# Fused transformer stack on one core: weight roundings issued one product earlier in attention, and units' steps put ahead of mixed rows' splits in the third layer

## The chip, the cores and the metric

One core of a Trainium2 chip. The metric is the device time of one execution in microseconds (us). Each kernel is run several times; the median is compared.

## The reference

Two blocks in sequence on 256 rows of width 1024, float32. The first has four layers of the kinds A, B, C, A:

```
q, k, v, (indexer), qm = x @ w_in
mix   = attention(rope(q), rope(k), v)      # A: top-64 keys by an indexer, B: dilated, C: causal
mo    = memory_attention(qm, mem_n @ w_mem_kv)
mixed = concat([mix, mo]) @ w_out
x     = layer_norm(ALPHA * x + mixed)
x     = layer_norm(ALPHA * x + swiglu(x, w_gate_up, w_down))
```

The second block has two layers of retention and stick-breaking attention. The change touches the attention of the four layers of the first block alone. They are called layer one to four here (0 to 3 in the code).

## The kernel before

A planner (class Plan) writes one list of steps; each engine's program then walks that list and issues its own part of each step. So the order of the list is the order on every engine, and every engine works strictly along its own queue, waiting on semaphores.

**Products.** Weights come as tiles of 128 x 2048 (half of the contraction for 512 output columns). A product is one tile against one block of 128 rows: 12 matmuls (L1309; L1303 and L1306 for transposed kinds), in three passes: rounded weights times rounded rows, rounded weights times the rows' remainder, the weights' remainder times rounded rows. Two halves make one result in a PSUM bank of a ring of two (`gemms`), which is then copied out: L1560 on ScalarE (ACT), L1920 on VectorE (DVE), by the `by` given in `some` (layer four copies the rows' values on ACT alone).

**Weights.** SyncE fetches tiles into three places of `w_raw`. Two steps make a tile usable. `high` (L1528, ACT) rounds it to `w_high`; `low` (L1777, DVE) writes the remainder `w_low`. `w_high` and `w_low` have five places each, so `high` of a tile waits for the last product of the tile five before it. `low` is cut in two where a unit's scores follow within one product (function `around`): the first half is L1777, the rest (`low_rest`, L1784) comes just after the step that masks the scores.

**Bookkeeping.** `owed` counts places that may be refilled now; `given_back` counts places that came free but are only added to `owed` at the next `split` or `settle`. A product that is `prompt` adds its place to `owed` at once. `split` issues the pending `low` steps and one `high`; `ahead` issues one `high`; `on` advances the background units and calls `split`.

**Units.** Attention runs as units of some heads on one block of 128 rows, advanced in the background between products, pipelined three deep. A unit's steps: scores (PE L1163); mask and maximum (DVE L2061, for memory L2039); exponentials (ACT L1604, L1612); reciprocals (DVE L2075); division of half of the heads on ACT (L1623) and half on DVE (L2085; the dilated kind adds three parts at L2078 and L2080 instead); transposition of the probabilities (PE L1376) into a ring of two PSUM banks (`tr`); copies of them to SBUF (DVE L2099); weighted sum of values (PE L1410 or L1402), which takes a bank of the same ring; its copy out (ACT L1648, dilated: DVE L2117). In the text the units of rows 0 are A0, B0 and M0 (memory), those of rows 1 are C1, C2, C3 (in layer two also C4) and M1.

**Mixed rows' split.** Before the output product the mixed rows are split into rounded rows and remainder: `mix_split`, ACT L1655 and DVE L2106, in halves (group 0 and group 1) for each block of rows. Layer two transposes them on PE first (L1238, L1537, L1811).

The order of products in `attention` and `out_and_forward` (layer three): values' last columns and memory queries, values' columns for rows 0 and rows 1 (`some`), then the output weights, four tiles W0 to W3 (columns 0 and 512 of the first half, then of the second), rows 0 then rows 1, then the first gate/up tile G0. Layers one and four have the memory queries between the values' products.

```
while self.used.get(self.oldest) == RB or ...:
    back = self.tiles[self.oldest].name != "w_ada_2"
    self.given_back, self.owed = self.given_back + (back and not prompt), self.owed + (back and prompt)
```

Of the kernel before, what the change touches and what calls it, by code (L numbers as in the profile page):

```python
# [150 lines left out]
class Plan:  # L151
# [624 lines left out]
    def attention(self, layer, gen, keys, values, tail):  # L776


        kind, mix = KINDS[layer], ("mix", layer)
        own = [self.own_units(layer, rb) for rb in range(RB)]  # L780
        mem = [self.memory_unit(layer, rb) for rb in range(RB)]
        ahead = 1 if kind == "A" else 0
        units = self.headed(own[0] + own[1][:ahead] + mem[:1] + own[1][ahead:] + mem[1:], 1)

        def begin():
            self.held = False
            self.on()
            self.drain()
            self.beside(units)
            self.step_background()  # L790

        def keys_turned(rb):
            def then():
                self.background[:] = [self.abreast(self.turn_heads(layer, "k", rb, 2 if kind == "A" and rb == 0 else 1),
                                                   *self.background)]
                self.step_background() if late else self.on()
            return then
        late = kind == "A" and layer
        self.group([keys], gen, [[self.on, keys_turned(0)], [self.step_background if late else self.on, keys_turned(1)]], True)
        if kind == "A":  # L800
            t = [self.tile(*values[:4], 4 * half) for half in range(2)]
            t_tail = [self.tile(tail[0], tail[1], None, "queries", 0)] * 2
        else:
            t_tail, t = [[self.tile(*what[:4], 4 * half) for half in range(2)] for what in (tail, values)]

        def some(n, tiles, where, sort, hooks):
            use = self.gemms.take()
            for half in range(2):
                self.gemm(tiles[half], n, half, gen, "gemm", use, sort)
                if half:  # L810
                    by = ("dve",) * 2 if where[0] == "qm" else ("act",) * 2 if where == ("proj", LAST, 3) else ("act", "dve")
                    self.evacuate(where, by=by)(n, use, tiles[half])
                hooks[half]()
            return use
        if kind != "A":
            self.blocks[("qm", layer), 0] = some(1, t_tail, ("tail", layer), "tail", [self.on, begin])
        some(0, t, ("proj", layer, 3), "block", [begin if kind == "A" else self.on, self.on])
        if kind == "A":
            some(0, t_tail, ("qm", layer), "queries", [self.on_ahead if layer == LAST else self.on, self.on])
        else:  # L820
            use = some(0, t_tail, ("tail", layer), "tail", [self.on] * 2)
            for rb in range(RB):
                self.blocks[("v", layer), rb] = use

        def first_turned():
            if kind == "A":
                self.step_background()
            self.xt(mix, 0, (0,))
            if kind == "C":
                self.on_ahead()  # L830
            else:
                self.split() if kind == "A" else self.on()

        def turned():
            if kind == "C":
                self.low_one()
            if kind != "A":
                assert len(self.units[layer, 0]) == len(own[0]) + 1
                self.xt(mix, 0, (1,))
            self.on()  # L840
        some(1, t, ("proj", layer, 3), "block", [first_turned, turned])

    def out_and_forward(self, layer):
# [2027 lines left out]
```

## Time and profile before

| | |
|---|---|
| median of 3 runs | 1554.36 us (1553.69 to 1554.85) |
| profiled execution | 1553.68 us |
| its span, first to last instruction | 1551.9 us |
| busy in the span: PE, DVE, ACT | 1528.5, 1088.2, 760.7 us |
| granted TensorE clock, mean | 0.999 |

Read the busy time of PE first, then where PE waits inside the attention stretches, then which engine's instruction ends each wait. An instruction's own time is the column after its start; the number in brackets is how long its engine had been idle before it and what ended that. Consecutive instructions of one engine can overlap by some 0.1 us, so the time that one takes from its engine is the distance between starts.

### The profile page before, as it was taken

What the parts mean: (1) busy time and instruction counts of PE and PEld (TensorE: products, weight loads), DVE (VectorE), ACT (ScalarE), POOL (GpSimd) and SP (SyncE); (2) the same over time, 40 slices, a digit from 0 to 9 for tenths busy, and PEclk for the clock granted to TensorE, in tenths of its full rate; (3) what the DMA queues carried; (4) which work ended last, traced back from release to release, by engine and by line L of the source; (5) the groups of instructions that cost most, each with busy time, mean ns of one, the idle gap of its engine ahead of it and who ended that gap; (6) DMA issues with size and microseconds to landing.
All of it is one profiled execution on the core that took longest, in us unless ns stands there. A gap on an engine that the chain in (4) does not pass through costs nothing.

```text
span 1551.9 us, 19840 instructions
## 1 busy us (share of the span) xinstructions
PE 1528.5 (98%) x8091; PEld 1267.8 (82%) x8091; DVE 1088.2 (70%) x1561; ACT 760.7 (49%) x963; POOL 52.1 (3%) x89
## 2 busy tenths in 40 slices
PE   9999999999999999999999999999999999999997
PEld 7887788888878888888788888877888888978986
DVE  6986866656777775676966756888667678567764
ACT  5657444444445443346544343566444434574463
POOL 1100000000000000000000000000100000000010
PEclk9999999999999999999999999999999999999999
DMA  8661666644435766352476654533766645433530
GB/s 320 245 231 55 226 224 264 249 174 179 163 104 201 262 261 243 138 215 83 178 252 234 244 225 148 204 109 136 267 257 236 223 166 223 164 118 140 217 122 27
DMA packets 45898, 299.87 MB, mean 193 GB/s; under 512 B 5540, under 2 KB 5796, under 8 KB 12528
## 3 DMA queue, kind: packets, MB, share of 16 engines
q1 hardware_dynamic: 39600, 278.74, 48.6%
q0 software_dynamic: 5776, 19.01, 3.7%
q8 instruction: 64, 1.05, 0.3%
q10 hardware_dynamic: 432, 0.85, 0.1%
q14 instruction: 26, 0.21, 0.0%
HBM read 296.20 MB, written 2.65 MB: 193 GB/s over the span
## 4 chain that ended last, share of the span: by engine, by line
PE 83%; DVE 9%; ACT 4%; issue 2%; DMA 0%; POOL 0%; POOLq 0%; SPq 0%; DVEq 0%; ACTq 0%
PE psum L1309 53%; PE psum L1268 15%; PE psum L1303 7%; DVE w_low L1777 3%; PE psum L1163 2%; PE psum L1238 1%; PE psum L1422 1%; ACT work L1604 1%; PE psum L1325 1%; ACT w_high L1528 1%; PE psum L1306 1%; DVE work L2061 1%; PE psum L1376 1%; DVE work L2099 1%; DVE xt_low L1811 0%
## 5 line engine op out<-in xcount | busy, mean ns | idle before, releaser
L1528 ACT ACTIVATE w_high<-w_raw 128x2048 fp32r<-128x2048 f32 (+1 forms) x240 | 456.4, 1903 | 230.7 <-DMA w_raw<-in_weights 144.9
L1777 DVE TENSOR_TENSOR w_low<-w_raw,w_high 128x2048 fp32r<-128x2048 f32 (+2 forms) x240 | 530.0, 2214 | 34.4 <-ACT w_high L1528 33.3
L1309 PE MATMUL psum<-w_high,xt_high 128*128 128x512 f32 (+1 forms) x1376 | 378.6, 395 | 1.4 <-DVE x_rows L1875 0.7
L1309 PE MATMUL psum<-w_high,xt_low 128*128 128x512 f32 (+1 forms) x1376 | 368.4, 388 | 0.3 <-DVE xt_low L1811 0.3
L1309 PE MATMUL psum<-w_low,xt_high 128*128 128x512 f32 (+1 forms) x1376 | 368.1, 388 | 0.0
L1309 PEld LDWEIGHTS psum<-w_high,xt_low 128*128 128x128 f32 x1376 | 257.4, 188 | 54.8 <-DVE xt_low L1811 0.7
L1309 PEld LDWEIGHTS psum<-w_low,xt_high 128*128 128x128 f32 x1376 | 257.3, 188 | 53.7 <-DVE w_low L1777 0.4
L1309 PEld LDWEIGHTS psum<-w_high,xt_high 128*128 128x128 f32 x1376 | 249.8, 188 | 52.5 <-DVE x_rows L1875 2.3
L2128 DVE TENSOR_TENSOR arena<-arena,psum 128x256 f32<-128x256 f32 x88 | 36.9, 420 | 205.4 <-ACT arena L1663 205.0
L1663 ACT ACTIVATE arena<-psum 128x256 f32<-128x256 f32 x88 | 33.7, 383 | 218.5 <-PE psum L1309 218.5
L1268 PE MATMUL psum<-w_high,ht_high 128*128 128x512 f32 x352 | 99.9, 401 | 0.0
L1268 PE MATMUL psum<-w_high,ht_low 128*128 128x512 f32 x352 | 96.1, 390 | 0.0
L1268 PE MATMUL psum<-w_low,ht_high 128*128 128x512 f32 x352 | 95.9, 390 | 0.0
L1268 PEld LDWEIGHTS psum<-w_high,ht_low 128*128 128x128 f32 x352 | 66.1, 188 | 14.4
L1268 PEld LDWEIGHTS psum<-w_low,ht_high 128*128 128x128 f32 x352 | 66.1, 188 | 14.1
L1268 PEld LDWEIGHTS psum<-w_high,ht_high 128*128 128x128 f32 x352 | 63.2, 188 | 11.0
L1560 ACT ACTIVATE arena<-psum 128x512 f32<-128x512 f32 (+1 forms) x54 | 30.4, 569 | 83.0 <-PE psum L1309 46.3
L1800 DVE SCALAR_TENSOR_TENSOR arena<-w_raw,c_col,arena 128x512 f32<-128x512 f32 x84 | 62.9, 749 | 2.6
L2364 POOL TENSOR_TENSOR norm_rstd<-norm_rstd,half_neg 128x1 f32<-128x1 f32 (+1 forms) x32 | 22.8, 715 | 1126.8 <-DVE norm_rstd L1860 871.2
L1604 ACT ACTIVATE work<-work,neg_max 128x128 f32<-128x128 f32 (+3 forms) x80 | 38.0, 477 | 28.2 <-DVE neg_max L2061 27.9
L1920 DVE TENSOR_SCALAR arena<-psum 128x512 f32<-128x512 f32 x25 | 17.2, 688 | 48.3 <-PE psum L1309 25.4
L1811 DVE TENSOR_TENSOR xt_low<-psum,xt_high 128x512 fp32r<-128x512 f32 (+1 forms) x48 | 31.0, 672 | 18.0 <-ACT xt_high L1537 17.5
(253 smaller groups left out, 1494.8 us busy)
## 6 DMA issues: line engine op xcount, KB each, us to landing
w_raw<-in_weights SPq DMA_DIRECT2D x260, 1024.0 KB, 4.8
norm_params<-in_ln_g POOLq DMA_DIRECT2D x8, 512.0 KB, 4.4
norm_params<-in_ln_b POOLq DMA_DIRECT2D x8, 512.0 KB, 5.9
w_raw<-in_weights SPq DMA_DIRECT2D x4, 656.0 KB, 6.1
kv_outside<-arena POOLq DMA_DIRECT2D x3, 512.0 KB, 4.5
mem_kv<-kv_outside POOLq DMA_DIRECT2D x3, 512.0 KB, 3.7
norm_params<-mods_outside POOLq DMA_DIRECT2D x3, 512.0 KB, 5.8
x_rows<-in_x SPq DMA_DIRECT2D x4, 256.0 KB, 5.6
```

Source lines behind the costliest of these rows:

```text
L1163: m = e.matmul(pieces[n][1], left, right, start=banks[i] not in banks[:i], stop=banks[i] not in banks[i + 1:])
L1268: m = e.matmul(psum[:, K.wide.place(j.use) + h, :], left[:, c, rb * P:rb * P + P], right[:, w:w + BLK], start=first and c == 0 and n == 0, ...
L1303: m = e.matmul(dst, right[:, c + b * P:c + b * P + P], rows[:, kk, :], start=first and b == 0, stop=last and b == 1)
L1309: m = e.matmul(psum[:, bank, 0:w], rows[:, kk, rb * P:rb * P + P], right[:, at:at + w], start=first, stop=last)
L1528: e.activation(K.w_hi[:, g % RING, 0:w], K.w_raw[:, r, 0:w], ACT.Copy).then_inc(K.high.hit(t), 1)
L1560: m = e.activation(to, out, ACT.Silu if j.silu else ACT.Copy, scale=K.evac_scale(j.where, j.rb))
L1604: m = e.activation(pr, pr, ACT.Exp, bias=K.negmax[:, slot, n:n + 1], scale=-1.0, accum_out=K.expsum[:, slot, n:n + 1])
L1663: e.activation(K.ff_silu[j.step % 2][:, j.rb, :], psum[:, K.gemms.place(j.use), 0:FF_STEP], ACT.Silu).then_inc(K.silu_done.hit((j.layer, j ...
L1777: m = e.tensor_tensor(K.w_lo[:, s, 0:n], K.w_raw[:, r, 0:n], K.w_hi[:, s, 0:n].bitcast(F32), ALU.subtract)
L1800: m = e.scalar_tensor_tensor(out=acc, in0=w, scalar=c, in1=acc, op0=ALU.mult, op1=ALU.add)
L1811: m = e.tensor_tensor(lo[at], psum[:, K.tr.place(j.use), 0:n * P].rearrange("p (c s) -> p c s", s=P), hi[at].bitcast(F32), ALU.subtract)
L2128: e.tensor_tensor(K.ff_h[j.step % 2][:, j.rb, :], K.ff_silu[j.step % 2][:, j.rb, :], bank[:, FF_STEP:BLK], ALU.mult).then_inc(K.gemms.sem( ...
```

## The change

In `some`, the products of the values and memory queries become `prompt`: their tiles' places are owed at once and not at the next `split`. So from there until the first gate/up tile each `high`, and with it its `low`, stands one product earlier in the list: W2, W3, G0 in layers one and four, W1, W2, W3, G0 in layers two and three. The list still has the same steps.

In layer three (kind C) also: the units are advanced before `mix_split` of group 0 and group 1 for rows 0, where they were advanced after it; the calls around them issue their `high` and `low` in the matching order.

```diff
         def some(n, tiles, where, sort, hooks):
             use = self.gemms.take()
             for half in range(2):
-                self.gemm(tiles[half], n, half, gen, "gemm", use, sort)
+                self.gemm(tiles[half], n, half, gen, "gemm", use, sort, prompt=True)
...
         def first_turned():
-            if kind == "A":
+            if kind != "B":
                 self.step_background()
             self.xt(mix, 0, (0,))
             if kind == "C":
-                self.on_ahead()
+                self.settle()
             else:
                 self.split() if kind == "A" else self.on()
 
         def turned():
             if kind == "C":
                 self.low_one()
+                self.ahead()
+                self.step_background()
             if kind != "A":
                 assert len(self.units[layer, 0]) == len(own[0]) + 1
                 self.xt(mix, 0, (1,))
-            self.on()
+            self.split() if kind == "C" else self.on()
```

The instructions of PE, GpSimd and SyncE stand in the same order as before; those of ACT and DVE move. Line numbers below the edit are two higher in the changed kernel (L1528 is L1530 there).

ACT in layer two, where M0's exponentials and division (L1612, L1623) are followed by the copy of the values' last columns (L1560, `arena` 128x2x256) and C1's exponentials (L1604); before:

```order
L1612 ACTIVATE work,exp_sum<-psum,neg_max 128x256 x4
L1623 ACTIVATE work<-work,recip 128x256 x2
L1560 ACTIVATE arena<-psum 128x2x256
L1604 ACTIVATE work,exp_sum<-work,neg_max 128x768
L1528 ACTIVATE w_high<-w_raw 128x2048
```

and in the changed kernel:

```order
L1614 ACTIVATE work,exp_sum<-psum,neg_max 128x256 x4
L1625 ACTIVATE work<-work,recip 128x256 x2
L1530 ACTIVATE w_high<-w_raw 128x2048
L1562 ACTIVATE arena<-psum 128x2x256
L1606 ACTIVATE work,exp_sum<-work,neg_max 128x768
```

The rounding of W1 has moved from behind C1's exponentials to ahead of the copy. Layer three has the same move at the same place.

ACT in layer four, from M0's division over the split of rows 0, group 0 (L1655), and the copy of the values' columns for rows 1 (L1560) to C1's copy out (L1648); before:

```order
L1612 ACTIVATE work,exp_sum<-psum,neg_max 128x256 x4
L1623 ACTIVATE work<-work,recip 128x256 x2
L1655 ACTIVATE xt_high<-arena 128x4x128
L1560 ACTIVATE arena<-psum 128x512
L1648 ACTIVATE arena<-psum 128x256
```

and in the changed kernel:

```order
L1614 ACTIVATE work,exp_sum<-psum,neg_max 128x256 x4
L1625 ACTIVATE work<-work,recip 128x256 x2
L1657 ACTIVATE xt_high<-arena 128x4x128
L1530 ACTIVATE w_high<-w_raw 128x2048
L1562 ACTIVATE arena<-psum 128x512
```

The rounding of W2 now stands between the split and the copy. In layer one it moves to the same place, but there the copy is DVE's.

DVE in layer three, from the copies of C1's probabilities (L2099) over C2's reciprocals and division to the masks of C3; L1920 copies the values' columns for rows 1; before:

```order
L2099 TENSOR_SCALAR work<-psum 128x512 x2
L2075 RECIPROCAL recip<-exp_sum 128x4
L2085 TENSOR_TENSOR work<-work,recip 128x512
L1920 TENSOR_SCALAR arena<-psum 128x512
L1777 TENSOR_TENSOR w_low<-w_raw,w_high 128x1024
L2106 TENSOR_TENSOR xt_low<-arena,xt_high 128x4x128
L2061 ISA work,neg_max<-psum,causal 128x256
```

and in the changed kernel:

```order
L1786 TENSOR_TENSOR w_low<-w_raw,w_high 128x1024
L2101 TENSOR_SCALAR work<-psum 128x512 x2
L2077 RECIPROCAL recip<-exp_sum 128x4
L2087 TENSOR_TENSOR work<-work,recip 128x512
L2108 TENSOR_TENSOR xt_low<-arena,xt_high 128x4x128
L1922 TENSOR_SCALAR arena<-psum 128x512
L1779 TENSOR_TENSOR w_low<-w_raw,w_high 128x1024
L2063 ISA work,neg_max<-psum,causal 128x256
```

The remainder of group 0, which stood ahead of C2's masks, now stands behind C2's division and ahead of the values' copy; the remainder of group 1 has left the place ahead of C3's masks. The halves of W1's remainder that stood around C3's masks are those of W2 now.

## Rows read from the trace of the kernel before

**Rows 1.** The page: busy time of the engines, and one group of instructions.

```profile
PE 1528.5 (98%) x8091; PEld 1267.8 (82%) x8091; DVE 1088.2 (70%) x1561; ACT 760.7 (49%) x963; POOL 52.1 (3%) x89
...
L1777 DVE TENSOR_TENSOR w_low<-w_raw,w_high 128x2048 fp32r<-128x2048 f32 (+2 forms) x240 | 530.0, 2214 | 34.4 <-ACT w_high L1528 33.3
```

**Rows 2.** Windows, attention of layers one to four: length, busy time, granted clock, DMA.

```profile
132.00:178.80 46.80, 45.38 (x295) 34.68 (x295) 38.95 (x69) 31.21 (x68) 1.10 (x2) 1.00 0.28 102
415.00:475.00 60.00, 57.67 (x332) 46.22 (x331) 44.54 (x79) 29.15 (x51) 1.09 (x2) 1.00 0.32 113
711.00:770.00 59.00, 56.03 (x389) 44.25 (x388) 44.97 (x91) 38.14 (x90) 1.09 (x2) 1.00 0.30 109
1005.00:1080.00 75.00, 73.31 (x484) 58.50 (x483) 64.78 (x168) 49.24 (x116) 0.55 (x1) 1.00 0.29 105
```

**Rows 3.** Waits of PE, whole span: line, releaser, us in total, times, longest.

```profile
PE psum L1376 <- ACT arena L1648: 2.3, 3, 1.2
PE psum L1410 <- DVE work L2099: 2.0, 2, 1.0
...
PE psum L1309 <- DVE x_rows L1875: 0.7, 2, 0.4
```

**Rows 4.** Timeline, ACT in layer one: start, us, instruction, idle time before.

```profile
143.42 0.39 ACT L1648 ACTIVATE arena<-psum 128x256 f32<-128x256 f32 x1 [2.31 <-PE psum L1410]
```

**Rows 5.** Timeline, DVE in layer one: masks of C3.

```profile
148.39 0.43 DVE L2061 CUSTOM_DVE_ANT_0 work<-psum,select_bias 128x256 f32<-128x256 f32 x1 [1.53 <-PE psum L1163]
```

**Rows 6.** Timeline, ACT in layer two: M0's division and the values' copy.

```profile
425.62 0.91 ACT L1623 ACTIVATE work<-work,recip 128x256 f32<-128x256 f32 x2 [0.25 <-DVE recip L2075]
426.44 0.58 ACT L1560 ACTIVATE arena<-psum 128x512 f32<-128x512 f32 x1
```

**Rows 7.** Timeline, PE in layer two: B0's weighted sum and M0's second transposition.

```profile
427.40 0.92 PE L1402 MATMUL psum<-arena,work 128*128 128x192 f32 x4
...
429.00 0.66 PE L1376 MATMUL psum<-ident,work 128*128 128x128 f32 x4 [0.24 <-DVE arena L2117]
```

**Rows 8.** Timeline, ACT in layer three.

```profile
721.50 0.91 ACT L1623 ACTIVATE work<-work,recip 128x256 f32<-128x256 f32 x2 [0.25 <-DVE recip L2075]
722.75 0.60 ACT L1560 ACTIVATE arena<-psum 128x512 f32<-128x512 f32 x1 [0.34 <-PE psum L1306]
...
728.48 1.90 ACT L1528 ACTIVATE w_high<-w_raw 128x2048 fp32r<-128x2048 f32 x1
730.28 0.61 ACT L1655 ACTIVATE xt_high<-arena 128x512 fp32r<-128x512 f32 x1
```

**Rows 9.** Timeline, PE in layer three: weighted sums, C2's scores, second transpositions.

```profile
723.71 0.88 PE L1410 MATMUL psum<-work,arena 128*64 128x128 f32 x12
...
728.53 1.13 PE L1163 MATMUL psum<-arena 64*128 64x256 f32 x8
...
736.70 0.88 PE L1410 MATMUL psum<-work,arena 128*64 128x128 f32 x12 [0.65 <-DVE arena L1920]
...
738.90 0.66 PE L1376 MATMUL psum<-ident,work 128*128 128x128 f32 x4 [0.73 <-ACT arena L1648]
...
746.16 0.66 PE L1376 MATMUL psum<-ident,work 128*128 128x128 f32 x4 [1.19 <-ACT arena L1648]
...
751.57 0.66 PE L1376 MATMUL psum<-ident,work 128*128 128x128 f32 x4 [0.39 <-ACT arena L1648]
```

**Rows 10.** Timeline, DVE in layer three: group 0's remainder, values' copy.

```profile
730.92 0.69 DVE L2106 TENSOR_TENSOR xt_low<-arena,xt_high 128x512 fp32r<-128x512 f32 x1 [2.57 <-ACT xt_high L1655]
...
735.96 0.68 DVE L1920 TENSOR_SCALAR arena<-psum 128x512 f32<-128x512 f32 x1
```

**Rows 11.** Chain that ended last, layer four: start, us, what.

```profile
1045.72 0.49 ACT arena L1560
...
1046.26 0.88 PE psum L1410 x12
...
1048.28 2.76 PE psum L1309 x12
```

## The prediction

> **What bounds the kernel now.** The page comes first: PE is busy for 98% of the span [rows 1]. The change adds and removes no instruction of PE, so it can only move PE's waits. How much of these lies where the change works, the windows of the four attention stretches say: 1.4, 2.3, 3.0 and 1.7 us without a busy PE, 8.4 us in 240.8, at a granted clock of 1.00 [rows 2]. That is 0.5% of the time, and no gain can be larger. The list of PE's waits then says what ends them: copies of units by ACT (L1648) and DVE (L2099), and a bank that a residual frees (L1875) [rows 3]. No wait on w_high or w_low of these tiles stands among the long ones: the roundings come in time today. So the question is not whether a weight is ready sooner, but what a rounding pushes back on ACT and DVE where it now stands. A measurement can tell about 0.2% from no change, 3.1 us.
>
> **The change, layer by layer.** Prices: a w_high takes ACT 1.80 us from start to next start (728.48 to 730.28 [rows 8]); a w_low takes DVE 2.2 us [rows 1], a half of it 1.1. DMA is no matter: the fetch of a tile waits for a w_low three tiles before, which only comes sooner, and each moved w_high still stands behind the end of the product that frees its place, by the order of the steps.
>
> *Layer one: -0.35 us.* The w_high of W2 falls where ACT sat idle 2.31 us before C1's copy out [rows 4], so its 1.80 cost nothing; the next two step into the places that W2 and W3 leave. On DVE the first half of W2's w_low falls into 1.53 us of idling ahead of C3's masks [rows 5], also for nothing. The second half comes behind these masks and before the copies of C2's probabilities: 1.1 us of w_low and 1.2 us of copies now stand between the masks and C3's reciprocals, where 2.1 us of exponentials on ACT stood before, so the chain behind is 0.2 us later. It ends in PE's 1.0 us wait for M1's copies (L2099), which grows to 1.2. Behind these copies a whole w_low (2.2 us) is gone, so the residual for which the first gate/up product waited (L1875) [rows 3] comes in time. The bank wait there is 0.35 by that row, some 0.55 between the end of the product at its steady pace and the next start. 0.2 - 0.55 = -0.35. If the cover of ACT's idling were gone, the 1.8 would land on C2's exponentials; that is part of the upper bound below.
>
> *Layer two: +1.4 us.* Here the w_high of W1 comes ahead of ACT's copy of the values' last columns. ACT goes from M0's division straight to that copy [rows 6], at 426.44, with no idle time to fill, so the copy starts at 428.24 and ends near 428.85. B0's weighted sum on PE, which reads these columns from its first matmul on, started at 427.40 [rows 7]; it starts 1.4 us later. What follows on PE (M0's second transposition, waiting for that sum's copy out by DVE at 429.00 [rows 7], the product, the transposition of the mixed rows) hangs on it and moves with it. ACT and DVE hang on PE in turn, through the scores and the transposed rows, so I find no place where the delay is taken up again before the feed-forward. At the end one w_low less stands before the residuals, but no product waited for those here.
>
> *Layer three: -1.1 us.* The same delay first: ACT had 0.34 us of idling before the copy [rows 8], so it comes 1.46 us later, ends near 724.75, and B0's weighted sum (723.71 [rows 9]), whose first third does not read these columns, stops for 0.75 us. Then the gain: C2's masks no longer wait for group 0's remainder (730.92, after 2.57 us of waiting for ACT [rows 10]). They started at 731.5, when the remainder was done; now they start when the scores are there, at 728.53 + 1.13 [rows 9] and the 0.75, which is 730.4: 1.1 us sooner. Four masks (1.5 us) put C2's exponentials at 731.9, and with their 2.1, a reciprocal (0.2) and the division (0.9, as at 721.50 [rows 8]) ACT gets to the split at 735.1, ends it at 735.7, and DVE's remainder at 736.3. The values' copy on DVE (735.96 [rows 10]) now stands behind it and starts at 736.35, so C1's weighted sum resumes at 737.0 where it did at 736.70 [rows 9]: PE is 0.3 late. ACT has then rounded W3 from 735.7 to 737.5 and is free when the sum ends at 737.8, where before its copy out came after a w_high and a split, 0.4 ahead of 738.90; so the second transposition that came at 738.90 [rows 9] has nothing to wait for, and PE is 0.6 ahead. At 746.16 the wait stays (division, split of group 1, w_high of G0 and copy out are one chain of the same length, started 1.1 sooner, with the split's 0.5 in it): still 0.55 ahead. Before 751.57 no w_high is left on ACT, so that wait goes too: 1.1 ahead, and it stays so, since the products behind wait for nothing.
>
> *Layer four: +1.45 us.* As layer one, -0.35, but here the copy of the values' columns is ACT's. It follows the split without a pause, and C1's weighted sum follows the copy at once, in the chain that ended last: 1045.72, 1046.26 [rows 11]. The w_high between split and copy puts 1.80 on that chain. 1.80 + 0.2 - 0.55 = 1.45.
>
> **The sum.** -0.35 + 1.4 - 1.1 + 1.45 = +1.4 us. The profiled execution took 1553.68, 0.7 below the median of the runs shown; it gives 1555.1, and the median 1554.36 + 1.4 = **1555.8**. The unknown is what each delayed copy costs: nothing if its reader comes late anyway, the whole 1.80 if it is late by all of it. From below, with the three copies free, layer two is 0, layer four -0.35 and layer three -1.85 (C2's masks at 729.7, 1.85 sooner): -2.55. From above, three times 1.80 with nothing won back in layer three: +5.4 - 0.35 + 0.2. I stay with the values in between, since the rows show ACT and PE back to back at two of the three places.
>
> The granted clock is 1.00, the 2.4 GHz level, in all four windows [rows 2] though PE waits there, up to 1.2 us at once at L1376 [rows 3]. The Trainium skill (TensorE: Matmul & The Clock Gate, "What's actually happening") says that the array's clock is throttled by default and that only activity releases it. No row here shows a wait that brought it down; by that rule a longer wait could.
>
> **The rivals.** *The copies are not missed (0.15).* For it: PE's queue has other work before each reader. Against: the readers follow at once in [rows 7, 11]. Time: 1554.36 - 2.55 = 1551.8.
>
> *Layer three wins nothing back (0.12).* The place is the values' copy on DVE behind the split. If ACT, with a w_high now ahead of M0's copy out and C2's exponentials, starts these no sooner than today, the split comes at the time of a division of today plus a split, the copy is some 1.5 us late, and PE loses 1.5 there where I have it gaining 1.1. It decides whether they start before 733.0 (masks at 731.5 and their 1.5). For it: DVE's 0.3 to the wrong side is already in my sum. Against: 2.57 us of idling on DVE before the remainder [rows 10]. Time: -0.35 + 1.4 + 1.5 + 1.45 = +4.0, 1558.4: slower.
>
> *The places are no sooner free (0.10).* Then each w_high waits on ACT until about its old time, the sum is near 0 and the time 1554.4. Against: the step list puts each behind the product that frees its place.
>
> *The clock falls (0.02).* In layer four the added wait of 1.8 us could let the clock fall to the 1.2 GHz level for one transposition and one product, from the sum's end at 1047.1 to 1051.0, 3.9 us (1046.26 and its 0.88, 1048.28 and its 2.76 [rows 11]), which would take twice as long: +1.4 + 3.9, 1559.7. The clock of 1.00 [rows 2] speaks against it. It is the rule named above that would do this.
>
> **How the numbers follow.** My forecast has 0.61. The likeliest time is 1555.8; one copy mis-set, up or down by about the 1.4 that layer two's costs, leaves it within 1554.4 to 1557.2. The range reaches from 1552.8, half-way to the free copies, to 1558.5, which takes in layer three without a gain; outside are most of the free copies and the clock. Within 0.2%, 1551.3 to 1557.5: forecast 0.59, places no sooner 0.10, free copies 0.09, layer three 0.02, together 0.80. Slower: layer three 0.10, forecast 0.02, clock 0.02, together 0.14. Faster: 0.06, from the free copies.
>
> **What would show it.** In the changed profile: in layer two and three ACT's w_high directly ahead of the copy L1562 and PE's L1404 or L1412 waiting for it, 1.4 and 0.7 us; in layer four a wait of about 1.8 before C1's sum, released by ACT L1562; in layer three C2's masks ahead of the split, and the waits for L1650 down from 2.3 us to about 1.2; in layers one and four no wait for the residual before the first gate/up product, and 1.2 us before M1's sum. Wrong would be: no wait on L1562 at all (then faster), the wait for L1650 undiminished (then slower), or any w_high waiting long for PE ahead of those copies.

## The result, and the profile after

The changed kernel takes 1559.15 us (median of 7 executions, 1558.15 to 1559.9) against 1553.94 for the kernel before (7 executions, 1553.67 to 1554.85), a ratio of 1.0033 with an interval of 1.0023 to 1.0043: slower by 5.2 us, where +1.4 was forecast and the range ended at 1558.5. The profiled execution took 1559.15 us with a span of 1557.3. One execution of all those reported here, of the kernel with scores done twice, ran in a slower state (1897.21 us at a mean granted clock of 0.752); without it that kernel's median is 1555.55 us and not 1555.83. In the rows of the changed kernel w_high is L1530, ACT's copy L1562, the weighted sums are L1404 and L1412, a unit's copy out is L1650.

The page's busy time of the changed kernel, to be held against [rows 1]:

```profile
PE 1532.2 (98%) x8091; PEld 1271.6 (82%) x8091; DVE 1089.5 (70%) x1565; ACT 760.3 (49%) x963; POOL 52.2 (3%) x89
```

This line tells most of the story. PE executes the same 8091 matmuls, but is busy 3.7 us longer (1532.2 - 1528.5). The span has grown by 5.4, so only 1.7 us of that are more waiting; the larger part is matmuls that take longer. What makes the same matmul longer is the clock. The windows of the four attentions (columns as in [rows 2], stretches cut a little differently) show it:

```profile
118.00:176.00 58.00, 56.90 (x400) 45.13 (x400) 44.74 (x102) 38.81 (x102) 1.10 (x2) 1.00 0.30 106
415.00:476.00 61.00, 57.45 (x325) 46.39 (x324) 44.02 (x78) 28.17 (x51) 1.09 (x2) 0.97 0.28 100
712.00:772.00 60.00, 57.96 (x396) 45.71 (x396) 46.56 (x94) 39.30 (x93) 1.09 (x2) 1.00 0.34 119
1017.00:1083.00 66.00, 62.53 (x424) 49.41 (x422) 53.66 (x122) 44.29 (x108) 0.55 (x1) 0.97 0.34 114
```

In layers two and four the granted clock is 0.97 where [rows 2] had 1.00. PE's waits, which answer to [rows 3]:

```profile
PE psum L1412 <- ACT arena L1562: 2.4, 2, 1.8
...
PE psum L1404 <- ACT arena L1562: 1.5, 1, 1.5
...
PE psum L1378 <- ACT arena L1650: 1.0, 1, 1.0
```

Three waits on ACT's copy (L1562) are new, 1.5 in layer two, 0.58 in layer three and 1.84 in layer four; the three waits for units' copies (L1650) have become one; the wait for a residual ahead of the first gate/up product is gone.

**Layer two.** ACT's timeline, which answers to [rows 6]: division, w_high, copy.

```profile
424.89 0.91 ACT L1625 ACTIVATE work<-work,recip 128x256 f32<-128x256 f32 x2 [0.24 <-DVE recip L2077]
425.70 1.90 ACT L1530 ACTIVATE w_high<-w_raw 128x2048 fp32r<-128x2048 f32 x1
427.50 0.57 ACT L1562 ACTIVATE arena<-psum 128x512 f32<-128x512 f32 x1
```

PE's timeline there, which answers to [rows 7]: the scores, B0's weighted sum, the transpositions, the product.

```profile
425.18 1.56 PE L1165 MATMUL psum<-arena 64*128 64x256 f32 x6
428.22 1.51 PE L1404 MATMUL psum<-arena,work 128*128 128x192 f32 x4 [1.48 <-ACT arena L1562]
429.52 1.97 PE L1378 MATMUL psum<-ident,work 128*128 128x128 f32 x8
431.15 1.45 PE L1311 MATMUL psum<-w_high,xt_high 128*128 128x512 f32 x4
```

And windows of 1 us (the last column but two is the granted clock):

```profile
427.00:428.00 1.00, 0.00 (x0) 0.00 (x0) 0.74 (x2) 1.00 (x3) 0.00 (x0) 1.00 0.00 0
428.00:429.00 1.00, 0.78 (x3) 0.81 (x4) 0.00 (x0) 1.00 (x4) 0.00 (x0) 0.67 0.00 0
429.00:430.00 1.00, 1.00 (x6) 0.91 (x5) 0.23 (x1) 1.00 (x1) 0.00 (x0) 0.50 0.00 0
...
431.00:432.00 1.00, 1.00 (x6) 0.85 (x5) 0.78 (x2) 0.00 (x0) 0.00 (x0) 0.62 0.00 0
432.00:433.00 1.00, 1.00 (x6) 0.83 (x5) 1.00 (x2) 0.00 (x0) 0.00 (x0) 1.00 0.00 0
```

PE stands still for 1.48 us, with the clock at 1.00, and begins again at 428.22. Some 0.1 us later the clock is 0.50, the 1.2 GHz level, and stays there until about 431.8 (both times worked out from these windows). The sum that took 0.92 us in [rows 7] takes 1.51. **Layer four** shows the same on PE, after 1.84 us:

```profile
1049.03 1.08 PE L1412 MATMUL psum<-work,arena 128*64 128x128 f32 x12 [1.84 <-ACT arena L1562]
1050.03 1.97 PE L1378 MATMUL psum<-ident,work 128*128 128x128 f32 x8
1051.65 1.77 PE L1311 MATMUL psum<-w_high,xt_high 128*128 128x512 f32 x4
```

Here the clock comes down about 0.5 us after PE has begun again and is back by 1053:

```profile
1049.00:1050.00 1.00, 0.97 (x12) 0.68 (x12) 0.00 (x0) 0.00 (x0) 0.00 (x0) 0.78 0.09 16
...
1052.00:1053.00 1.00, 1.00 (x4) 0.79 (x3) 0.93 (x3) 0.63 (x3) 0.00 (x0) 0.51 0.00 0
1053.00:1054.00 1.00, 1.00 (x6) 0.80 (x5) 1.00 (x2) 1.00 (x3) 0.00 (x0) 1.00 0.00 0
```

**The second block**, where the change moves nothing, holds a third such stretch. PE's timeline of the changed kernel, and a window behind its two waits:

```profile
1290.03 0.66 PE L1240 MATMUL psum<-ident,work 128*128 128x128 f32 x4 [1.08 <-DVE work L2187]
1291.42 0.69 PE L1240 MATMUL psum<-ident,work 128*128 128x128 f32 x4 [0.73 <-DVE work L2187]
1291.83 1.99 PE L1311 MATMUL psum<-w_high,xt_high 128*128 128x512 f32 x4
1293.62 1.88 PE L1311 MATMUL psum<-w_high,xt_low 128*128 128x512 f32 x4
```

```profile
1292.00:1294.00 2.00, 2.00 (x6) 1.56 (x6) 1.27 (x4) 0.60 (x1) 2.00 (x4) 0.50 0.31 77
```

Four matmuls of a product take 1.99 and 1.88 us here, 1.17 and 1.08 at full clock. The kernel before has the same two waits 3.77 us earlier, at 1286.26 and 1287.64, and its window behind them is at 1.00:

```profile
1288.00:1290.00 2.00, 2.00 (x12) 1.66 (x11) 1.30 (x3) 0.60 (x1) 1.83 (x4) 1.00 0.27 69
```

The starts of the same work on PE in the two profiles give a ledger (us; the last column is by how much the difference grew since the row above):

| work on PE | before | changed | difference | step |
|---|---|---|---|---|
| layer one, scores | 118.18 | 117.96 | -0.22 | start of the program |
| layer one, second transposition for gate/up | 187.10 | 186.41 | -0.69 | -0.47, layer one |
| layer two, sum ahead | 421.98 | 421.25 | -0.73 | |
| layer two, B0's weighted sum | 427.40 | 428.22 | +0.82 | +1.55, wait |
| layer two, transposition of the mixed rows | 432.26 | 434.28 | +2.02 | +1.20, clock |
| layer three, scores | 705.80 | 707.63 | +1.83 | |
| layer three, second transposition for gate/up | 778.93 | 779.78 | +0.85 | -0.98, layer three |
| layer four, scores | 1044.68 | 1045.68 | +1.00 | |
| layer four, next scores | 1050.97 | 1055.17 | +4.20 | +3.20: wait 1.84, clock 1.36 |
| layer four, second transposition for gate/up | 1090.87 | 1094.58 | +3.71 | -0.49 |
| second block, waiting transposition | 1286.26 | 1290.03 | +3.77 | |
| second block, turning after the products | 1293.62 | 1299.02 | +5.40 | +1.63, clock |
| near the end | 1529.88 | 1535.33 | +5.45 | |

The three stretches at half clock cost 1.20 + 1.36 + 1.63 = 4.19 us. The 1.20 is what is left after the 0.24 us wait of [rows 7], which is gone. In layer four 1.84 is PE's idle time; by the starts of the waiting sum (1046.26 in [rows 11], 1049.03 here) the split would be 1.77 of wait and 1.43 of clock. Without the stretches the layers come to -0.47 + 1.55 - 0.98 + (1.84 - 0.49) = +1.45.

### The profile page after: what moved, and what is told of

Same layout as the page of the kernel before. It is cut to its first block, busy times and chain, and to the rows that moved or that the text cites. A ratio compares the mean times of both kernels' runs of the same rounds, so it can differ in the third digit from the quotient of the medians.

```text
span 1557.3 us, 19847 instructions
## 1 busy us (share of the span) xinstructions
PE 1532.2 (98%) x8091; PEld 1271.6 (82%) x8091; DVE 1089.5 (70%) x1565; ACT 760.3 (49%) x963; POOL 52.2 (3%) x89
## 4 chain that ended last, share of the span: by engine, by line
PE 84%; DVE 8%; ACT 4%; issue 2%; DMA 1%; SPq 0%; POOL 0%; POOLq 0%; ACTq 0%; DVEq 0%
PE psum L1311 54%; PE psum L1270 15%; PE psum L1305 7%; DVE w_low L1779 2%; PE psum L1165 2%; PE psum L1240 1%; PE psum L1424 1%; ACT w_high L1530 1%; PE psum L1327 1%; PE psum L1378 1%; DMA w_raw<-in_weights 1%; DVE work L2101 1%; PE psum L1412 1%; PE psum L1308 1%; DVE work L2063 1%
## 5 line engine op out<-in xcount | busy, mean ns | idle before, releaser
L1530 ACT ACTIVATE w_high<-w_raw 128x2048 fp32r<-128x2048 f32 (+1 forms) x240 | 456.5, 1903 | 229.4 <-DMA w_raw<-in_weights 136.1
L1562 ACT ACTIVATE arena<-psum 128x512 f32<-128x512 f32 (+1 forms) x54 | 30.4, 568 | 83.5 <-PE psum L1311 46.3
L1539 ACT ACTIVATE xt_high<-psum 128x512 fp32r<-128x512 f32 (+1 forms) x48 | 26.7, 586 | 35.0 <-PE psum L1240 34.7
```

Source lines behind the costliest of these rows:

```text
L1530: e.activation(K.w_hi[:, g % RING, 0:w], K.w_raw[:, r, 0:w], ACT.Copy).then_inc(K.high.hit(t), 1)
L1539: m = e.activation(hi[:, 4 * j.g:4 * j.g + n, j.rb * P:j.rb * P + P], psum[:, K.tr.place(j.use), 0:n * P].rearrange("p (c s) -> p c s", s= ...
L1562: m = e.activation(to, out, ACT.Silu if j.silu else ACT.Copy, scale=K.evac_scale(j.where, j.rb))
```

## The experiments

Theory A: PE's standing still at the new waits brings the clock down, and this costs more than the waits. Rival B: the low clock belongs to the new order or to the execution as a whole. Rival C: the new order is needed, a wait alone is not enough. All ratios are against the kernel before in the same series (medians 1554.07 to 1554.47).

**Take the waits away.** In a copy of the change, the three w_high that stand ahead of ACT's copies are put behind them, by a pass over the finished list of steps (the numbers are those of the tiles; 75, 128, 185 are the first moved ones of layers two, three and four):

```diff
-        self.steps = steps
+        self.steps = copies_first(steps, (75, 128, 185))
...
+def copies_first(steps, moved):
+    steps = list(steps)
+    for t in moved:
+        at = steps.index(("high", t))
+        to = next(n for n in range(at, len(steps)) if steps[n][0] == "evac" and steps[n][1].by == "act")
+        steps.insert(to, steps.pop(at))
+    return steps
```

> The change with three steps swapped: in layers two, three and four the w_high that stands directly ahead of ACT's copy of the values' columns comes directly behind it. Theory A (each of those waits costs its own length, and in layers two and four the lower clock behind it as well): layer one keeps its -0.47 us, layer two gives about 0, layer three -1.0 to -1.85 since its 0.75 us wait is gone too, layer four -0.47; together -1.9 to -2.8 us against the kernel before, 1551.1 to 1552.0 us, or 1.6 more if the fall of the clock at the second block's start stays. The windows of 428 to 432 and 1049 to 1053 us show the clock at 1.00. Rival B (the lower clock belongs to the new order as a whole, not to these waits): the waits on ACT's copy go but the three stretches at half clock stay, 4.2 us in all: 1555.3 us or more.

Measured: 1553.34 us, ratio 0.9994 (0.9985 to 1.0003), which is not clear of no change and above the 1551.1 to 1552.0 expected. No window of PE's work is at half clock any more, near 428, 1049 or 1290 us; rival B, that the new order as a whole lowers the clock, falls.

```profile
428.00:430.00 2.00, 1.76 (x13) 1.41 (x12) 1.85 (x5) 2.00 (x4) 0.00 (x0) 1.00 0.00 0
...
1048.00:1050.00 2.00, 2.00 (x11) 1.59 (x9) 1.40 (x4) 1.75 (x7) 0.00 (x0) 1.00 0.00 0
...
1288.00:1290.00 2.00, 2.00 (x11) 1.63 (x10) 1.97 (x4) 0.00 (x0) 1.21 (x3) 1.00 0.75 258
```

In its profile layer three gave -1.33, layer one -0.53. Layer four missed the expectation: +0.25 instead of -0.47. PE's timeline there says why:

```profile
1046.95 0.65 PE L1378 MATMUL psum<-ident,work 128*128 128x128 f32 x4 [0.61 <-ACT arena L1650]
```

Behind the copy the w_high stands ahead of C1's copy out (L1650), which a transposition waits for. Neither of the two places tried on ACT in layer four is free.

In the next kernel only layer two's w_high goes behind the copy:

```diff
+        self.steps = copies_first(steps, (75,))
```

> The change with one step swapped: in layer two alone the w_high comes behind ACT's copy; layers three and four keep their waits. Theory A: layer two's +2.75 us go (1.5 of wait, 1.2 of lower clock) and layer four's 1.8 us wait with its 1.4 us of lower clock stays: 1559.15 - 2.75 = 1556.4 us. If the third stretch at half clock, at the second block's start, needs the falls before it or the exact time at which its waits are met, it may go as well: 1554.8. Rival B: only the 1.5 us of the wait go, 1557.7 us, and the clock falls near 428 us as before.

Measured: 1555.66 us, ratio 1.0010 (1.0001 to 1.0019); the profiled execution took 1556.7. Layer two is at 1.00; layer four has its wait (1.89 us) and the low clock behind it; the second block falls too. Layer four's fall does not need layer two's. PE's windows in layer four:

```profile
1046.00:1048.00 2.00, 1.23 (x14) 1.05 (x15) 0.54 (x4) 1.02 (x4) 0.00 (x0) 0.88 0.00 0
1048.00:1050.00 2.00, 2.00 (x10) 1.90 (x9) 1.10 (x2) 2.00 (x9) 0.00 (x0) 0.50 0.00 0
```

One profile shows one execution, and the executions of a kernel differ. The mean granted clock, which is known for all of them, runs from 0.996 (the profiled one and two more) to 0.999 in the 11 of this kernel, and their times from 1553.39 to 1557.61 us. By the ledger a fall in layer four alone gives 1555.5 us and one in the second block as well 1557.1 (estimates): the median fits the first, the profile the second.

**Keep the late copies, but keep PE working.** The sharpest test leaves the change as it is and gives PE more to do: the scores directly ahead of the two waiting sums are computed twice.

```diff
-        m = accumulate(e, score_pieces(K, j.wide, n_pieces, nk, j.kind == "dil"), work)
+        for _ in range(2 if (j.layer, j.rb, j.heads) in ((1, 1, (0,)), (LAST, 1, (4, 5, 6, 7))) else 1):
+            m = accumulate(e, score_pieces(K, j.wide, n_pieces, nk, j.kind == "dil"), work)
```

> The changed kernel, in which PE does the scores of two units twice (the same values into the same banks): those that stand directly ahead of the waiting weighted sums in layers two and four, 6 and 8 matmuls, about 1.4 and 1.0 us more work. The late copies stay as they are, so the sums begin no sooner, but PE idles some 0.1 us there instead of 1.48 and some 0.8 instead of 1.84. Theory A (PE's idling lowers the clock): the clock stays at 1.00 at both places and more work takes less time: 1559.15 - 1.2 - 1.4 = 1556.5 us, and 1554.9 if the second block's start keeps its clock too. Rival B (the late copies cost this time whatever PE does): 1559.2 us; if the masks behind the longer scores come late as well, 1 to 2 us more.

Measured: 1555.83 us, ratio 1.0009 (1.0000 to 1.0018), profiled 1555.08: some 3.5 us less than the changed kernel, with 14 matmuls more. The page's busy time, and PE's timeline at both places:

```profile
PE 1530.5 (99%) x8105; PEld 1269.4 (82%) x8105; DVE 1089.4 (70%) x1565; ACT 761.1 (49%) x963; POOL 52.3 (3%) x89
```

```profile
425.87 2.85 PE L1165 MATMUL psum<-arena 64*128 64x256 f32 x12
428.92 0.89 PE L1405 MATMUL psum<-arena,work 128*128 128x192 f32 x4 [0.20 <-ACT arena L1563]
...
1048.51 0.88 PE L1413 MATMUL psum<-work,arena 128*64 128x128 f32 x12 [1.02 <-ACT arena L1563]
1049.32 1.21 PE L1379 MATMUL psum<-ident,work 128*128 128x128 f32 x8
1050.29 1.17 PE L1311 MATMUL psum<-w_high,xt_high 128*128 128x512 f32 x4
```

8105 matmuls keep PE busy for 1530.5 us, where the changed kernel's 8091 took 1532.2. The sums start as late as before, but sum and transposition take 0.89 and 1.21 us again instead of 1.51 and 1.97: the clock stayed at 1.00. The second block kept its clock too, which is some 1.6 of the 3.5 us. By the starts, layer two now loses 1.5 us and layer four 1.8 up to the next scores: the waits alone.

**Make the wait alone, in the kernel before.** Nothing is moved; layer four's copy on ACT is cut into more and more pieces, so that only C1's weighted sum is late. With 8 pieces (64 columns), 16 (32), 24 (22) and 32 (16); the edit for 16:

```diff
-        for to, out in zip(K.evac_to(j.where, j.rb), K.evac_from(j)):
+        pairs = list(zip(K.evac_to(j.where, j.rb), K.evac_from(j)))
+        if (j.where, j.rb) == (("proj", LAST, 3), 1):
+            pairs = [(to[:, c:c + BLK // 16], out[:, c:c + BLK // 16]) for to, out in pairs for c in range(0, BLK, BLK // 16)]
+        for to, out in pairs:
```

> The kernel before with layer four's copy in 8 pieces of 64 columns: about 0.15 us each, 1.2 us for 0.5, so C1's weighted sum waits about 0.7 us, as long as layer three's 0.75 us wait in the changed kernel, where the clock stayed at 1.00. Theory A: +0.7 us and clock 1.00: 1554.9 us. If any added wait at that place lowers the clock: 1556.3 us.

> The kernel before, in which one instruction is made longer and nothing is moved: layer four's copy of the values' columns on ACT is done in 16 pieces of 32 columns. By the rows of that kind (512 columns 0.52 us from start to start, 384 columns 0.37, 256 columns 0.28) a piece takes about 0.12 us, the copy 1.9 us for 0.5, and C1's weighted sum waits some 1.4 to 1.8 us, as in the changed kernel. Theory A (the wait itself lowers the clock): half clock from about 1048 us for one transposition and one product, +1.4 us: 1554.2 + 1.6 + 1.4 = 1557.2 us, and 1558.8 if the second block's start falls too. Rival C (the new order of the roundings is needed for it): clock 1.00 and 1555.8 us.

> The kernel before with layer four's copy on ACT in 24 pieces of 22 columns (the last one 6). The 16 pieces took 1.48 us and made C1's weighted sum wait 0.96 us, so a piece costs 0.09 us, and 8 more make the wait 1.7 us, about the 1.84 us of the changed kernel, with no rounding moved. Theory A (a wait of that length at that place lowers the clock): half clock from about 1048 us for the transposition and the product, and 1554.4 + 1.7 + 1.4 = 1557.5 us. Rival C (the new order of the roundings is needed): clock 1.00 there and 1556.1 us. The second block's start may fall or not in both, 1.6 us.

> The kernel before with layer four's copy on ACT in 32 pieces of 16 columns. 16 pieces made C1's weighted sum wait 0.96 us, 24 pieces 1.48, both at clock 1.00; by 0.065 us a piece it waits 2.0 us here, more than the changed kernel's 1.84. If the length of PE's stop decides at this place (between 1.48 and 1.84): half clock from about 1048 us, and 1554.1 + 2.0 + 1.4 = 1557.5 us. If the new order of the roundings is needed for it: clock 1.00 and 1556.1 us.

| pieces | PE's stop | clock behind it | median | ratio |
|---|---|---|---|---|
| 8 | 0.5 | 1.00 | 1554.0 | 0.9998 (0.9990 to 1.0007) |
| 16 | 0.96 | 1.00 | 1555.2 | 1.0006 (0.9997 to 1.0015) |
| 24 | 1.48 | 1.00 | 1555.7 | 1.0010 (1.0001 to 1.0019) |
| 32 | 1.99 | 0.50 | 1557.32 | 1.0019 (1.0010 to 1.0028) |

The waits were guessed too high: 0.7 us for 8 pieces, 1.4 to 1.8 for 16, 1.7 for 24. So the stops with 16 and 24 pieces stayed shorter than the changed kernel's 1.84, the clock stayed up, and by the expectations as written these two came out on rival C's side; that is why the series was carried on. PE's timeline with 24 pieces:

```profile
1049.07 0.88 PE L1410 MATMUL psum<-work,arena 128*64 128x128 f32 x12 [1.48 <-ACT arena L1563]
1049.88 1.21 PE L1376 MATMUL psum<-ident,work 128*128 128x128 f32 x8
```

its window behind the stop:

```profile
1050.00:1051.00 1.00, 1.00 (x9) 0.87 (x10) 0.42 (x1) 1.00 (x4) 0.00 (x0) 1.00 0.00 0
```

and the same two views with 32:

```profile
1048.10 0.88 PE L1410 MATMUL psum<-work,arena 128*64 128x128 f32 x12 [1.99 <-ACT arena L1563]
1048.91 1.67 PE L1376 MATMUL psum<-ident,work 128*128 128x128 f32 x8
```

```profile
1050.00:1051.00 1.00, 1.00 (x5) 0.90 (x4) 0.73 (x2) 1.00 (x5) 0.00 (x0) 0.50 0.00 0
```

With 32 pieces the median came out at 1557.32 where 1557.5 was expected with the fall and 1556.1 without. The profiled execution, 1558.68 us, has the second block's stretch as well. Layer two, with its copy in 29 pieces:

```diff
...
+        if (j.where, j.rb) == (("tail", 1), 0):
+            pairs = [(to[:, :, c:min(c + 9, BLK // 2)], out[:, :, c:min(c + 9, BLK // 2)]) for to, out in pairs for c in range(0, BLK // 2, 9)]
...
```

> The kernel before with layer two's copy of the values' last columns on ACT in 29 pieces of 2 x 9 columns (the last 2 x 4), so that B0's weighted sum waits about as long as the 1.48 us of the changed kernel, with no rounding moved; by 0.065 us a piece over the 0.96 us that 16 pieces cost in layer four, and 0.2 us of slack there, 1.5 to 1.9 us. If a stop of that length at that place is enough: half clock from 428 us for the sum and the transposition, and 1554.1 + 1.5 + 1.2 = 1556.8 us or a little more. If the new order is needed: clock 1.00 and 1555.6 to 1556.0 us.

Measured: 1556.82 us, ratio 1.0015 (1.0007 to 1.0024), and PE's timeline:

```profile
429.05 1.51 PE L1402 MATMUL psum<-arena,work 128*128 128x192 f32 x4 [1.41 <-ACT arena L1563]
430.36 1.97 PE L1376 MATMUL psum<-ident,work 128*128 128x128 f32 x8
```

A stop of 1.41 us, with no rounding moved, gives the same 1.51 and 1.97 as the change did. Rival C falls at both places.

**The third stretch.** Is it fixed by the program, by the exact time, or met by chance? The changed kernel was run once more, unedited:

> The changed kernel once more, nothing edited. If the three stretches at half clock are fixed by the program, they stand again near 428, 1049 and 1292 us and the time is 1559.1 us. If what brings the clock down is met by chance from execution to execution, one or two of them are missing here or lie elsewhere, and the time is 1.2 to 1.6 us lower for each that is missing.

Measured: 1559.4 us, ratio 1.0032 (1.0020 to 1.0045); all three stretches stand again, and all 12 executions of the changed kernel lie between 1558.02 and 1559.9 us. The kernel before was shifted in time:

```diff
-        for c in range(2 if stage == "mix" and g else 4):
+        for c in list(range(2 if stage == "mix" and g else 4)) * (7 if (j.gen, rb, g) == (("ff", 0), 0, 0) else 1):
```

> The kernel before, in which the first four transpositions of layer one's feed-forward rows are done seven times instead of once (the same values into the same bank): 24 transpositions more, at 0.15 us (1.21 us for 8) 3.6 us, so that everything behind is met 3.6 us later, as in the changed kernel at the second block's start; no other instruction moves and no wait is added. If the third stretch at half clock comes from the time at which the second block's waits of about 1.1 and 0.7 us are met: a stretch at half clock near 1296 us and 1553.9 + 3.6 + 1.6 = 1559.2 us. If it comes from the falls before it, or from the changed order: clock 1.00 there and 1557.5 us.

Measured: 1556.32 us, ratio 1.0013 (1.0004 to 1.0022), clock 1.00. The 24 transpositions took 2.6 us, 0.11 each where 0.15 was reckoned (32 in 3.41 us from start to next start, 8 in 0.79 before), and 0.7 us of it came back up to the second transposition for gate/up, where among others the 0.35 us wait for the residual is gone. So the second block is met only 1.4 us later, and the shift did not reach the changed kernel's 3.77. It told something all the same: the second block's first wait ended at 1287.70 here with full clock behind it, and at 1287.64 in the kernel with layer two's copy first, where the clock fell. The time since the program's start does not decide. The kernel before was also run again:

> The kernel before once more, nothing edited. If the fall of the clock at the second block's start is met by chance and belongs to no edit, some executions of this kernel have it too: the times lie in two heaps, near 1553.5 and 1.5 us higher, and the profiled one may show half clock near 1289 us. If it belongs to the changed order, the times lie in one heap and the clock is 1.00.

Measured: 1553.91 us, ratio 1.0003 (0.9994 to 1.0012), 11 executions from 1553.1 to 1556.81, the profiled one (1554.79) at clock 1.00. That is inconclusive: of its own 1.1 us over the first profile 0.85 are there after 53 us of the program, so times alone do not tell a low clock. The mean clock of its 11 executions is 0.998 or 0.999; but of the 102 executions of the kernel before in these series 15 have 0.997, and they take 1554.62 to 1557.51 us, so a low stretch in some of them can't be excluded. Of all 14 profiles of this study five have the third stretch: the four whose clock fell in layer four, and the kernel with 16 pieces, whose clock had not fallen before:

```profile
1288.00:1290.00 2.00, 1.28 (x6) 1.19 (x7) 1.34 (x2) 0.79 (x2) 0.76 (x2) 0.71 0.58 246
1290.00:1292.00 2.00, 2.00 (x6) 1.61 (x5) 1.56 (x3) 0.41 (x1) 1.43 (x3) 0.50 0.64 209
```

So the order of the change isn't needed for it, nor is a fall before it; but a fall in layer four was followed by it four times in four, and its absence by it once in ten. In the profiles, that is: the medians with layer two's copy first (1555.66) and with 32 pieces (1557.32) fit a fall in layer four without it. What links them was not settled.

**The change without its losses.** The change in layers one and three alone, layer three's first w_high behind the copy (`copies_first` as above):

```diff
-                self.gemm(tiles[half], n, half, gen, "gemm", use, sort, prompt=True)
+                self.gemm(tiles[half], n, half, gen, "gemm", use, sort, prompt=layer in (0, 2))
...
-        self.steps = steps
+        self.steps = copies_first(steps, (128,))
```

> The change in layers one and three alone, with layer three's first moved w_high directly behind ACT's copy; layers two and four as before. By the two traces and the copy-first run: layer one -0.5 us, layer three -1.3 us (there -0.17 to -1.50 from its first product to its first gate/up product), layers two and four 0: 1554.2 - 1.8 = 1552.4 us with the clock at 1.00 throughout. The rival, that any sooner rounding costs its length somewhere on ACT, gives 1554.2 or more.

Measured: 1552.4 us, as expected, ratio 0.9988 (0.9979 to 0.9997). By the starts layer one gives 0.5 and layer three 1.4 us. That is some 2 us under the kernel before, with an interval that just excludes no change, but inside the 0.2% that a measurement is said to tell: faster than the changed kernel, and likely but not firmly faster than the kernel before.

## Why the prediction was wrong

Its sum was right and its time was not: +1.4 forecast for what the moved instructions do, +1.45 by the ledger without the clock; the clock added 4.2, which stood in the sum as nothing, with a chance of 0.02. Some 1.6 of that is the second block's stretch, whose cause is open; without it the time would have been about 1557.5, inside the range.

*Layer one, -0.35 forecast, -0.47 measured.* The wait for the residual is gone, as said. M1's wait for its copies did not grow from 1.0 to 1.2; by the starts M1's sum comes 0.1 us later and not 0.2, which is most of the difference.

*Layer two, +1.4 forecast, +1.55 measured up to B0's sum.* The mechanism was as said: w_high between division and copy, the sum waiting 1.48 us for it.

*Layer three, -1.1 forecast, -0.98 measured.* The sum stopped 0.58 us where 0.75 was expected. C2's masks start at 732.33, which is 730.5 when the 1.83 us are taken off by which the layer began late; 730.4 was forecast. The values' copy stops C1's sum for 0.44 us, the waits at 738.90 and 751.57 [rows 9] are gone, the one at 746.16 is left with 1.01. The rival that layer three wins nothing back did not come.

*Layer four, +1.45 forecast, +1.35 measured without the clock.* The wait is 1.84 us, and 0.49 are won back at the feed-forward.

*The copies not missed, the places no sooner free:* neither came; all three copies were waited for, and every w_high found its place free.

*The clock.* The step that failed is the clock's term, left out of the sum: the sum priced each late copy as a wait alone, on matmuls of unchanged length, and the rival that said otherwise got a chance of 0.02. The text argued that the clock was 1.00 in all four windows "though PE waits there, up to 1.2 us at once". But the sum itself added stops of 1.4 and 1.8 us, longer than any of [rows 3]: rows on shorter stops said nothing about them. Nor was 1.2 the longest: inside layer two's window PE stops for 1.66 us at 453.74, at a clock of 1.00 (the row stands in the last section). That row would have spoken for the low chance too, so lengths alone would not have saved the forecast. What the profiles show at these two places: in layer four 1.48 us left the clock up in the one profile with such a stop, 1.84 to 1.99 brought it down in four profiles of four; in layer two 1.41 to 1.49 did in three of three. A border in length is not shown by this: 1.41 us lowered the clock in one place and 1.48 did not in another, and it was not tried whether the moment at which the stop is met decides with it, as the differences between executions of one kernel suggest.

The rival's place and price were off as well. It named layer four alone and doubled all of 1047.1 to 1051.0, 3.9 us. Measured are 1.36 us there, because the clock came down only about 0.5 us after PE had begun again and was back by 1053: of the chain behind the wait the transposition (1.97 for 1.21) and one product group (1.77 for 1.17) were slow. And two more stretches came that it did not name, 1.20 in layer two and 1.63 in the second block, so that the whole was close to its 3.9 by accident.

The Trainium skill (TensorE: Matmul & The Clock Gate, "What's actually happening") says that activity is what releases the throttle. By that rule PE's stop, and not the late copy, costs the clock; the runs agree, most plainly the one with the scores done twice, whose 14 extra matmuls left the clock at 1.00.

## What to carry to other kernels

When a step is moved ahead of another on a side engine, add up the stops that this makes for PE and hold them against the longest stops that the trace shows at full clock and in like surroundings: behind a stop that no such row covers the matmuls can be slower too (here by 1.2 to 1.6 us a stretch), and nothing in a sum of waits shows that. A busy time that grows while the count of matmuls stays is the first sign of it. Where a late operand can't be avoided, work on PE ahead of it, even repeated work, can be cheaper than an idle array, as the 14 extra matmuls were here.

## What the runs showed of the hardware

The clock comes down behind a stop, not in it. In the 12 stretches at half clock in layers two and four and the second block it fell 0.1 to 1.3 us after PE had begun again (worked out from windows of 1 us). So which matmuls are slow differs: in the second run of the changed kernel layer two's sum, 1.51 us long in the first, took 0.98 us and the fall came only towards its end.

```profile
428.40 0.98 PE L1404 MATMUL psum<-arena,work 128*128 128x192 f32 x4 [1.49 <-ACT arena L1562]
```

The length of a stop alone does not decide. In layer two PE stops for 1.66 us in every one of the 14 profiles, the kernel before among them, longer than the 1.41 to 1.49 us that brought the clock down 25 us earlier, and the clock stays at 1.00. In the kernel before, PE's timeline and the windows around it:

```profile
453.74 0.66 PE L1238 MATMUL psum<-ident,arena 128*128 128x128 f32 x4 [1.66 <-DVE arena L2117]
```

```profile
452.00:454.00 2.00, 0.34 (x3) 0.26 (x3) 2.00 (x4) 1.60 (x7) 0.00 (x0) 1.00 0.16 66
454.00:456.00 2.00, 2.00 (x12) 1.70 (x11) 0.89 (x3) 1.73 (x5) 0.00 (x0) 1.00 0.78 188
```

What differs is what PE did ahead of it: between the last scores and this stop stand a sum and a transposition; ahead of the stops that lowered the clock the scores come last in layer two, and scores and the first four matmuls of the sum (0.44 us) in layer four. Whether that is the reason was not tried. One more stretch stands in the profile with 24 pieces, at the program's start, where nothing was edited: PE waits 1.28 and 0.34 us there, and from 8 to 10 us the clock is 0.56 (the kernel before waits 0.55 and 0.34 us and stays at 1.00). And two short stops close together, 1.07 and 0.73 us with one group of transpositions (0.66 us) between them, lowered it in five profiles and left it in nine.
